# A decoder step on one core: router and expert rows computed from the raw residual, prompt states and one gate moved among the branches

## What is computed

```python
z = rmsnorm(x, norm_mix) @ w_in                    # ux, uy, q, k, v, g, mq, gates ga, gb, gc
a_out = rg_lru_branch(...) @ w_branch_lru
o, s_new = retention(rotary(q), rotary(k), v, s_prev)     # s_new: prompt state and 8 decode states
o = o * rsqrt(mean(o * o) + EPS)                   # per head
b_out = (silu(g) * o) @ w_branch_ret
c_out = cross_attention(...) @ w_branch_mem
merged = sigmoid(ga) * a_out + sigmoid(gb) * b_out + sigmoid(gc) * c_out
x = x + merged @ w_out
xn2 = rmsnorm(x, norm_ffn)
grp = argmax(xn2 @ w_grp + b_grp); top2 = top_k(softmax((xn2 @ w_exp_router + b_exp_router)[grp]), 2)
x = x + sum over the 2 chosen experts of weight * (silu(xn2 @ w_gate) * (xn2 @ w_up)) @ w_down
y = rmsnorm(x, norm_final)
```

## Time and profile before

| | |
|---|---|
| median of three runs | 1172.71 us |
| the profiled execution, its own time | 1173.44 us |
| its span, first to last instruction | 1171.6 us |
| PE busy with matmuls | 961.7 us, 82% of the span |
| DVE, ACT, POOL busy | 366.6, 221.4 and 100.9 us |
| read from HBM, written | 320.48 MB, 22.20 MB |
| chain that ended last, by engine | PE 47%, SP's queue 22%, DMA 20%, DVE 5% |

### The profile page before, as it was taken

One profiled execution on the slowest core, in us unless ns is written; L12 is line 12 of the kernel. 1 busy time (PEld: TensorE's weight loads), 2 busy tenths in 40 slices (PEclk: granted clock), 3 DMA queues, 4 the chain that ended last, 5 costly groups with the idle time before them and its releaser, 6 DMA issues.

```text
span 1171.6 us, 16329 instructions
## 1 busy us (share of the span) xinstructions
PE 961.7 (82%) x6950; PEld 705.9 (60%) x6950; DVE 366.6 (31%) x681; ACT 221.4 (19%) x453; POOL 100.9 (9%) x122
## 2 busy tenths in 40 slices
PE   7999999999999888999999888566647667675655
PEld 6888888768876666788888645333324333333323
DVE  3303573376223224452111362111162111111113
ACT  2112124114331222241000142010101011010102
POOL 0001121000123332100000140000000000000000
PEclk9999999999999999999999999998988888889897
DMA  9874466694569799745347949999999999999991
GB/s 318 277 251 153 158 216 229 191 278 124 201 231 307 245 299 317 255 144 181 108 144 274 372 167 416 417 417 417 417 417 415 418 416 417 415 418 416 416 404 62
DMA packets 138825, 343.80 MB, mean 293 GB/s; under 512 B 7640, under 2 KB 91864, under 8 KB 122360
## 3 DMA queue, kind: packets, MB, share of 16 engines
q1 hardware_dynamic: 124288, 290.05, 65.7%
q0 software_dynamic: 14464, 52.68, 13.3%
HBM read 320.48 MB, written 22.20 MB: 292 GB/s over the span
## 4 chain that ended last, share of the span: by engine, by line
PE 47%; SPq 22%; DMA 20%; DVE 5%; issue 4%; ACT 2%; POOL 1%; DVEq 0%; ACTq 0%; POOLq 0%
PE psum L961 28%; SPq L783 22%; DMA out_ret_s<-arena 10%; DMA arena<-in_w_up 8%; PE psum L693 3%; PE psum L1015 3%; PE psum L970 2%; PE psum L1027 2%; PE psum L703 2%; PE psum L677 1%; ACT arena L1301 1%; DVE arena L1664 1%; DMA arena<-arena 1%; POOL arena L866 1%; DMA arena<-in_state_ret 1%
## 5 line engine op out<-in xcount | busy, mean ns | idle before, releaser
L961 PE MATMUL psum<-arena 128*128 128x264 f32 x2048 | 473.6, 388 | 0.0
L961 PEld LDWEIGHTS psum<-arena 128*128 128x128 f32 x2048 | 387.6, 191 | 76.3 <-issue 12.0
L693 PE MATMUL psum<-arena 128*32 128x256 f32 x2048 | 148.4, 440 | 119.0 <-DMA arena<-in_w_up 118.1
L693 PEld LDWEIGHTS psum<-arena 128*32 128x32 f32 x2048 | 79.0, 123 | 181.8 <-issue 158.0
L1301 ACT ACTIVATE arena<-psum 128x264 f32<-128x264 f32 (+5 forms) x160 | 67.5, 439 | 350.8 <-PE psum L961 269.0
L1965 DVE SCALAR_TENSOR_TENSOR arena<-arena,psum 128x128 f32<-128x128 f32 x32 | 9.2, 288 | 237.0 <-ACT arena L1510 237.0
L1301 ACT ACTIVATE arena<-arena 128x1024 f32<-128x1024 f32 (+7 forms) x67 | 58.7, 903 | 106.7 <-DVE arena L1819 84.8
L703 PE MATMUL psum<-arena 128*32 128x256 f32 x1024 | 66.4, 402 | 11.8 <-ACT arena L1522 11.7
L1772 DVE SCALAR_TENSOR_TENSOR arena<-arena 128x512 f32<-128x512 f32 x64 | 45.6, 774 | 82.0 <-ACT arena L1301 81.9
L1229 PE MATMUL psum<-arena 128*128 128x264 f32 x112 | 40.1, 441 | 24.1 <-DVE arena L1977 24.1
L703 PEld LDWEIGHTS psum<-arena 128*32 128x32 f32 x1024 | 31.2, 115 | 41.3 <-ACT arena L1522 21.9
(11 more groups left out here) (246 smaller groups left out, 738.1 us busy)
## 6 DMA issues: line engine op xcount, KB each, us to landing
arena<-in_w_gate SPq DMA_DIRECT2D x64, 1024.0 KB, 22.8
arena<-in_w_up SPq DMA_DIRECT2D x64, 1024.0 KB, 22.5
arena<-in_w_down SPq DMA_DIRECT2D x64, 1024.0 KB, 22.9
arena<-in_w_in SPq DMA_DIRECT2D x48, 1024.0 KB, 5.4
arena<-in_state_ret POOLq DMA_DIRECT2D x16, 1024.0 KB, 7.1
out_ret_s<-arena POOLq DMA_DIRECT2D x16, 1024.0 KB, 9.3
arena<-in_w_mem_kv SPq DMA_DIRECT2D x8, 1024.0 KB, 11.6
arena<-in_cache_mem_k POOLq DMA_DIRECT2D x8, 1024.0 KB, 5.6
```

The costliest lines, as they stand in the source:

```text
L693: mm = pe.matmul(psum[32 * a:32 * a + SLOTS, bank, 0:256], tokens[:, 4 * half + k, SLOTS * j:SLOTS * (j + 1)], w[:, :, k, P * a:P * (a + 1 ...
L961: mm = pe.matmul(ps(task)[:, 0:T], w[:, k, (i % 2) * P:(i % 2 + 1) * P], rhs[:, k, :], start=k == 0, stop=k == KT - 1 and not two)
```

## The change

- `gb` joins the branches in the state stage, and so do the 8 pieces of the prompt's state, now tasks `("S", h, i)`: two 128 x 512 matmuls on PE, a copy and a 256 KB store on ACT (its own DMA issue). `prompt_state` is gone from the route.
- The four norms are woven over the first of the `g` projections; DVE's part of a `g` task is a task of its own, `gev`, one place later.
- `v_rows` and `k_rows` lie in ordinary buffers, so that all 18 weight tiles are free after the state stage. SP loads the three first experts in order, without a break.
- The router's weights are scaled with `norm_ffn` once (in `conv`). The logits and the sums of squares are computed from the raw `x_res` inside the `x2` stage (`router_part`); the token factor, and after it the bias, is applied to the logit rows. `xnT` is no longer written here.
- The rows are products of the raw residual with diagonal matrices of `norm_ffn` (24 matmuls), and ACT applies the factor as it copies them (24 copies). They stay fp32; the split into three parts, POOL's subtractions among it, is gone, and the gather is 24 fp32 matmuls with an fp32 `Sb`.
- DVE's choice of group and experts takes fewer, wider operations; ranks start at 1 and empty slots at 0; the token weights are computed behind the first one-hot matrix.
- The gather signals by halves (`gather_half`) and the tokens are taken by halves; the first `scatter_matrix` stands behind the first `gate_up`.

```diff
-                (LATE * CHUNK, LATE * CHUNK + 2 * HEADS * DV, stage["rows"], stage["end"]),
-                (LATE * CHUNK + 2 * HEADS * DV, TILES * CHUNK, stage["v"], stage["end"])]
+        held = [(0, RING1 * CHUNK, 0, stage["end"]), (RING1 * CHUNK, TILES * CHUNK, stage["ret"], stage["end"])]
...
+        ret += [("S", h, i) for i in range(2)]
...
-    branches = t("ga", 8) + t("lru_out", 8) + t("gc", 8) + t("mem_out", 8)
+    branches = t("ga", 8) + t("lru_out", 8) + t("gc", 8) + t("mem_out", 8) + t("gb", 8)
...
-    onorm = [("soT",), ("oq", 0), ("oq", 1), ("on", 0), ("oq", 2), ("on", 1), ("oq", 3), ("on", 2), ("on", 3)]
+    norms = {0: [("oq", 0)], 1: [("oq", 1), ("on", 0)], 2: [("oq", 2), ("on", 1)], 4: [("oq", 3), ("on", 2)],
+             6: [("on", 3)]}
+    gated = [("soT",)]
+    for i in range(VT):
+        gated += norms.get(i, []) + [("g", i)] + ([("gev", i - 1)] if i else [])
+    gated += [("gev", VT - 1)]
...
-        + weave(t("gb", 8), onorm) + t("g", 16) + t("ret_out", 8) + t("x2", 8) + [("x2_sq",)]
+        + gated + t("ret_out", 8) + t("x2", 8)
...
+        def router_part(pe, k):
+            if k == 0:
+                pe.wait_ge(router_scaled, 1)
+                read(pe, ("so", 0))
+            read(pe, ("x2", k))
+            pe.matmul(psum[0:NLOG, 7, 0:T], rout[:, k, :], x_res[:, k, :], start=k == 0, stop=k == KT - 1)
+            pe.wait_ge(squares, SQUARES + k + 1)
+            return pe.matmul(psum[64:96, 7, 0:T], ones[:, 0:32], sq3[:, k, :], start=k == 0, stop=k == KT - 1)
...
+            router_part(pe, KT - 2)
+            router_part(pe, KT - 1).then_inc(logitsT_full, 1)
+            pe.wait_ge(logitsT_ready, 1)
+            for t in range(TT):
+                mm = pe.transpose(psum[:, 2, t * P:t * P + 96], lgT[0:96, t * P:(t + 1) * P], ident[0:96, 0:96])
+            mm.then_inc(logits_full, 1)
...
-                pe.wait_ge(x2_normed, k + 1)
-                mm = pe.matmul(psum[0:NLOG, 3, 0:T], rout[:, k, :], xnT[:, k, :], start=k == 0, stop=k == KT - 1)
...
-                    mm = pe.transpose(psum[0:n, u % 2, k * P:(k + 1) * P], xnT[:, 4 * k4 + k, t * P:t * P + n], ident)
+                pe.wait_ge(diag_built, k + 1)
+                if k >= 4:
+                    pe.wait_ge(row_taken, k - 3)
+                for t in range(TT):
+                    n = rows_in(t)
+                    mm = pe.matmul(psum[0:n, row_bank(k), t * P:(t + 1) * P], x_res[:, k, t * P:t * P + n], diag[:, k, :],
+                                   start=True, stop=True)
                 mm.then_inc(row_full, 1)
-                for s in {3: (0, 1), 4: (2, 3), 5: (4, 5, 6, 7)}.get(u, ()):
-                    prompt_state(pe, s)
-                if u == 1:
...
-                    for x in range(3):
-                        mm = pe.matmul(psum[:, 5 + k // 4, (k % 4) * P:(k % 4 + 1) * P], xr[x][:, t, k * P:(k + 1) * P],
-                                       Sb[:, t, :], start=t == 0 and x == 0, stop=t == TT - 1 and x == 2)
-            return mm
+                    n = rows_in(t)
+                    mm = pe.matmul(psum[:, 5 + k // 4, (k % 4) * P:(k % 4 + 1) * P], xr[0:n, t, k * P:(k + 1) * P],
+                                   Sb[0:n, t, :], start=t == 0, stop=t == TT - 1)
+            if j % 2:
+                mm.then_inc(gather_half, 1)
...
-            for e, i in [(0, i) for i in range(6)] + [(1, 5), (2, 0), (2, 1), (2, 2)] + [(1, i) for i in range(5)]:
-                s = tile_at(e, i)
-                if s < RING1:
-                    full(sp, last_task[max(n for n in range(NCH) if n % RING1 == s)])
-                sp.dma_start(into(s, i), expert_part(e, i)).then_inc(chunk_loaded[s], 16)
-            for n in range(2 * HEADS):
-                h, i = divmod(n, 2)
-                sp.wait_ge(state_kept, n + 1)
-                sp.dma_start(outs["ret_p"][h, i * P:(i + 1) * P, :], kept_state(h, i)).then_inc(s_out, 16)
-            sp.wait_ge(s_out, 16 * 2 * HEADS)
-            for i in range(3, PARTS):
-                s = tile_at(2, i)
-                sp.dma_start(into(s, i), expert_part(2, i)).then_inc(chunk_loaded[s], 16)
+            for e in range(3):
+                for i in range(PARTS):
+                    s = tile_at(e, i)
+                    if s < RING1:
+                        full(sp, last_task[max(n for n in range(NCH) if n % RING1 == s)])
+                    sp.dma_start(into(s, i), expert_part(e, i)).then_inc(chunk_loaded[s], 16)
...
+            full(pool, ("ret_out", KT - 1))
...
-                        residual_squares(task[1] - 2)
+                        router_part(pe, task[1] - 2)
...
+                elif kind == "S":
+                    _, h, i = task
+                    if i == 0:
+                        read(pe, ("kr", 1, 1))
+                    begin(task)
+                    for m in range(2):
+                        mm = pe.matmul(ps(task)[:, 0:DV], k_rows[:, m, (2 * h + i) * P:(2 * h + i + 1) * P],
+                                       v_rows[:, m, h * DV:(h + 1) * DV], start=m == 0, stop=m == 1)
+                    end(task, mm)
...
-            pe.wait_ge(row_low, 2 * TT)
-            pe.wait_ge(onehot16_built, 1)
-            pe.wait_ge(state_kept, 2 * HEADS)
+            pe.wait_ge(slots_built, 1)
             for j in range(4):
-                mm = gather_part(pe, j)
-            mm.then_inc(gather_full, 1)
-            pe.wait_ge(onehot_built, 1)
-            scatter_matrix(pe).then_inc(scatterT_full, 1)
+                if j % 2 == 0:
+                    pe.wait_ge(row_taken, 2 * j + 4)
+                gather_part(pe, j)
...
+                if j == 0:
+                    pe.wait_ge(tokens_ready, 2 * q + 2)
...
+                if e == 0:
+                    pe.wait_ge(onehot_built, 1)
+                    scatter_matrix(pe).then_inc(scatterT_full, 1)
                 if q + 1 < QUADS:
-                    if j == 0:
-                        pe.wait_ge(onehot16_built, q + 2)
-                    mm = gather_part(pe, j)
+                    parts = (j,) if q else ((), (0, 1), (2,), (3,))[j]
+                    if 0 in parts:
+                        pe.wait_ge(slots_built, q + 2)
+                    for part in parts:
+                        gather_part(pe, part)
                     if j == 3:
...
+                elif kind == "S":
+                    _, h, i = task
+                    n = 2 * h + i
+                    full(act, task)
+                    if n >= 2:
+                        act.wait_ge(s_out[n % 2], 16 * (n // 2))
+                    run(S_st[:, n % 2, :], ps(task), ACT.Copy, free_of(task))
+                    steps.settle()
+                    act.dma_start(outs["ret_p"][h, i * P:(i + 1) * P, :], S_st[:, n % 2, :]).then_inc(s_out[n % 2], 16)
...
+                        run(rcol[:, 4:5], eps_col[:, 0:1], ACT.Sqrt)
...
+            act.wait_ge(logits_full, 1)
+            run(rcol[:, 0:TT], psum[:, 2, 64:64 + 2 * P + 1:P], ACT.Sqrt, root_cols, scale=1.0 / D, bias=eps_col[:, 0:1])
+            act.wait_ge(rstd_cols, 1)
+            for k in range(KT):
+                act.wait_ge(row_full, k + 1)
+                for t in range(TT):
+                    n, at = rows_in(t), 512 * (k // 4) + 32 * (k % 4)
+                    by_row = xr[0:n, t, 512 * (k // 4):512 * (k // 4) + 512].rearrange("t (j q) -> t j q", j=4)
+                    run(by_row[:, :, 32 * (k % 4):32 * (k % 4) + 32],
+                        psum[0:n, row_bank(k), t * P:(t + 1) * P].rearrange("t (q j) -> t j q", j=4), ACT.Copy,
+                        row_taken if t == TT - 1 else None, scale=rcol[0:n, t:t + 1])
+            act.wait_ge(router_exp_in, 1)
+            run(ex_in, ex_in, ACT.Exp, router_exp)
...
+            def take_tokens(a, done):
+                for b in range(2):
+                    act.wait_ge(gather_half, done + b + 1)
+                    A.activation(XgT[:, a, 4 * b:4 * b + 4, :].rearrange("p k s -> p (k s)"), psum[:, 5 + b, :],
+                                 ACT.Copy).then_inc(tokens_ready, 1)
...
+                    did(V.tensor_tensor(rout, rout, bc(cvs("norm_ffn").unsqueeze(2), (P, KT, NLOG)), ALU.mult),
+                        router_scaled)
...
+                    if i == 0:
+                        states_stored(dve)
+                        did(V.memset(Rc, 0.0))
+                        did(V.memset(Wc, 0.0))
+                        did(V.memset(lgT[0:96, T:TT * P], 0.0))
+                    if i < KT - 1:
+                        for k in range(i, KT if i == KT - 2 else i + 1):
+                            did(V.tensor_scalar(diag[:, k, :], ident, cv("norm_ffn", k), None, ALU.mult), diag_built)
...
+            v(V.tensor_copy(lgT[0:96, 0:T], psum[0:96, 7, 0:T]), logitsT_ready)
+            dve.wait_ge(root_cols, 1)
+            v(V.reciprocal(rcol[:, 0:TT], rcol[:, 0:TT]), rstd_cols)
...
+            sh_ge = (P, TT, G, E8)
```

(2 more changed lines are left out.)

342 lines of the change are left out of this document (125 added, 217 removed).

## The result

The changed kernel takes 1163.82 us (median of 4 runs, 1162.54 to 1165.52) against 1172.58 for the kernel before on the same chip. The ratio is 0.9926, with a 95% interval of 0.9911 to 0.9942. It is 8.8 us faster. The forecast was 22.4 us faster, 1150.3 us, in a range of 1142 to 1159. So the direction was right and the size was not: 13.5 us are missing, and the time lies above the range.

A forecast was written before the change was run, and what follows sets the result against it. The prediction took the unbroken expert-weight stream as the bound, so only the hole ahead of it could be won: +0.5 for R, -23.2 for the hole, +0.3 for router weights, -22.4 from 1172.7: 1150.3 us, range 1142 to 1159.

The forecast's parts named there:

- the sign named for being wrong: Among the conditions for being wrong: the first expert starts later than R + 56; 49 us after R was forecast.
- R: Start of the first residual product on PE, from which the route is counted; 628.34 before the change, 628.8 forecast.
- The frame: End is the moment the expert-weight stream runs unbroken, plus tiles still to come at 2.53 us each, plus an unchanged tail.
- the 19th tile: Expert-weight tile issued when the first half of gate and up products starts, ending the hole; forecast at R + 50.6.
- The state stage: PE sets the pace: 169.0 us plus 2 for single gaps, last half's product ending at 496.2, 18.1 later than before.
- The stall at the norm: PE waits 6.3 us in front of the first norm's sum, for the last state store; bounds 3 and 10.
- The route: Stretch from R through router, row products and gather to the first expert; 19th tile at R + 50.6.
- Eight residual products 28.5 us; 16 small products, 0.44 each, 7.0: Start of the route on PE: residual products with the router's small products among and behind them, ending at 35.5.
- PE's row products, 24 x 0.22 = 5.3, lie beside it: Route: PE's row products take 5.3 us beside ACT's block copies, which end at 43.8; the gather starts at 43.5.
- The gather, 24 at 0.22, 5.3: Route: the gather's 24 products at 0.22 take 5.3 us on PE, from 43.5 to 48.8 after R.
- The rival: Waits bring 1.2 GHz in the route; gather and first half expert take twice 5.3 and 1.8: +7.1, 1157.4 us, chance 0.22.
- DVE's chain: Route: 22 small operations at 0.18 plus handover, some 5 us; at 1.13 each for half, 10 us more.

The follow-up runs named there:

- r1: Changed kernel with the router's small products in pairs, two logit products then two of row sums behind every second residual product; 1159.59 us.
- c5: Changed kernel, first norm not awaiting the last store, useless products before the gather, ranks earlier, gather split, router products paired, third tile mostly padded to 128; 1145.40 us.
- k1: w3 with the third token tile gathered as 128 rows, of which 120 are zero; 1154.1 us, executed once.
- w4: Changed kernel with three bf16 products of 256 columns behind each of the eight groups of row products, both waits left empty; 1161.27 us.
- k2: Changed kernel with the third token tile gathered as 128 rows, 120 of them zero, and no filled wait; 1154.1 us.
- l1: w3 with the first gather taking 64 of its 128 columns, experts 2 and 3 getting no tokens; 1160.1 us, executed once.
- g2: Changed kernel whose first gather reads the upper 16 bits as bf16, one pass instead of fp32's two; 1155.54 us.
- w3: Changed kernel with 10 bf16 products of no use filling PE's wait in front of the gather; 1155.04 us.

## Why the prediction was half right

The time, 1163.8 us, lies above the range of 1142 to 1159, and the sign named for being wrong came: the first expert starts at R + 62.6, later than R + 56.

**The frame held.** The end is the 19th tile plus a rest that no run moved by more than 1.5 us from 468.1. From the prediction's 477.05 - 7.59 it should have been 469.5; the 1.4 us less in the kernel after were not traced.

**The state stage held.** The last half's product ended at 493.4, 496.2 forecast: none of the 2 us left for waits was needed, and 0.8 more was won. The stall at the norm was 6.33 for 6.3. What the step missed is that the stall takes the clock: 2.1 us more (1.25 - 0.61 and 5.17 - 3.72). The two misses nearly cancel, which is luck: 628.8 - 2.8 + 2.1 = 628.1, and 627.64 was read, within what R scatters.

**The route is the step that failed**, with R + 66.3 for R + 50.6. By its own terms:

- "Eight residual products 28.5 us; 16 small products, 0.44 each, 7.0": they end at R + 38.4, not R + 35.5. The small ones took 0.565 each (+2.0), as they alternate between 36 and 32 columns and between two places in PSUM; r1 gets part of it back. No run tells the two apart. A residual product behind one takes 3.76 instead of 3.56 (+1.0).
- "PE's row products, 24 x 0.22 = 5.3, lie beside it": they took 7.6, and the ranks stand behind them on PE. DVE's masks were ready at 672.93, R + 45.3 (the row below), the row products ended 1.7 us later. So they set the start of the gather, R + 48.7 instead of 43.5: 3.0 from the logits, 1.7 from the row products, and 0.5 more in the masks, the ranks and their handovers. Of the 2.3 us that the products ran over, 0.6 were hidden behind the masks. Eight of the 24 have 8 columns of weights beside 128; c5, with 128 columns for seven of these, took 0.232 each. That here too it is the change and not the 8 columns, the kernel before suggests: its four transposes of 8 columns one behind the other (at 678.54) take 0.44 us from start to start, 0.11 each, and eight of 128 columns, from 669.49 to 670.51, take 0.13 each.

```profile
672.67 0.26 DVE L1849 TENSOR_TENSOR arena<-arena 128x96 bf16<-128x96 f32 x1
```

```profile
669.49 1.09 PE L638 MATMUL psum<-arena 128*128 128x128 f32 x8
670.51 0.34 PE L646 MATMUL psum<-arena 36*128 36x36 f32 x3
...
678.54 0.60 PE L638 MATMUL psum<-arena 128*8 128x128 f32 x4 [2.15 <-ACT arena L1301]
678.98 3.60 PE L621 MATMUL psum<-arena 128*128 128x512 f32 x8
```

- "The gather, 24 at 0.22, 5.3": 8.5 at full clock, +3.2. Here the price was taken from a row of a 128 x 128 product and laid on products of 8 rows. k1 shows it right for 128 rows (5.62 for 24) and wrong for 8 in turn with 128 (0.58).
- The low clock: 13.97 - 8.49 = 5.5 in the gather and 1.8 in the first half, 7.3 together. The rival had 7.1 for it, at a chance of 0.22; it came true, and on top of what it did not know. That the two figures are so near is partly luck: the rival doubled a gather of 5.3 us, while one of 8.5 lost 5.5 from 1.5 us after its start on.

3.0 + 1.7 + 0.5 + 3.2 + 7.3 = 15.7 us. DVE's chain, the term I was least sure of, did not decide: its operations took 0.17 to 0.32 us, none the 1.13 of the earlier trace rows. What made that one long wasn't tested.

**The wait and the clock.** The Trainium skill (TensorE: Matmul & The Clock Gate, section "HAM oscillation — how this bites in real kernels") was weighed by its rule that short runs between waits start at the low clock. The waits in that section's example are several times as long as those of 1 to 2 us here, so the rule did not make this rival the likelier, as the prediction says it does. In the kernel after the gather did not start at the low clock either, but lost it 1.5 us in. w4 and k2 have the same wait of 1.0 and 1.3 us and keep 1.00, and l1 loses the clock without that wait. The runs show a sum of sparse work and wait, not the wait. k2 also ties the two errors together: with the shapes alike the gather keeps the clock by itself, and one edit brings the 19th tile from R + 66.3 to R + 56.5. It is not that this gather is short, for g2's was shorter. So the 8-row tile cost 3.2 us by itself and 7.3 through the clock.

## What to carry to other kernels

The price of a short product on PE is that of its sequence, not of its shape: take it from a row in which the neighbours have the shapes that they will have, and suspect every ragged last tile that stands in turn with full ones. Padding it with zeros to the full shape made 24 products 34% shorter here. Where a chain of short products decides, count it also at 1.2 GHz, and ask what the engine does just before it. And where a stall of several us is forecast on PE, add the slow products behind it.

## What the runs showed of the hardware beyond that

- An fp32 product of 8 rows between products of 128 rows costs 0.58 us, one of 128 rows 0.23; products with 8 columns of weights in turn with 128 cost (7.6 - 16 x 0.232) / 8 = 0.49. Padding to the full shape removed both.
- Products of no use gained time: 10 of 256 columns in bf16, 1.2 us of PE in a wait of 1.0, took 7 us off the route.
- Half the columns can cost the clock: l1's gather took longer than w3's (9.06 for 8.49 us) though it had half the columns, since the granted clock fell to 0.50 on the way (one execution).
